# The gate columns of the second block: from 24 split matmuls to eight column-tiled ones and one 0/1 sum

## The reference, cut to what matters

```
def hybrid_layer(x, norm_w, w_in, conv_w, conv_b, gate_bias, ret_norm_w, mlstm_norm_w, w_out):
    h = rmsnorm_2(x, norm_w)                       # x: 256 tokens of 1024
    proj = jnp.matmul(h, w_in)
    (aq, ak, av, ag, bq, bk, bv, bg, cq, ck, cv, co, cg, ci, cf) = jnp.split(proj, cuts, axis=-1)
    ...
    i_pre = ci.transpose(0, 2, 1) + gb[:C_HEADS][None, :, None]    # 4 columns
    f_pre = cf.transpose(0, 2, 1) + gb[C_HEADS:][None, :, None]    # 4 columns
    yc = mlstm(..., i_pre, f_pre)
```

## Time and profile before

| | us |
|---|---|
| median of 3 runs | 901.94 |
| lowest and highest | 900.82, 901.98 |
| the profiled execution | 900.98 |
| its span, first to last instruction | 899.7 |

### The profile page before, as it was taken

One profiled execution on the slowest core, in us unless ns is written; L12 is line 12 of the kernel. 1 busy time (PEld: TensorE's weight loads), 2 busy tenths in 40 slices (PEclk: granted clock), 3 DMA queues, 4 the chain that ended last, 5 costly groups with the idle time before them and its releaser, 6 DMA issues.

```text
span 899.7 us, 12205 instructions
## 1 busy us (share of the span) xinstructions
PE 855.5 (95%) x5030; PEld 554.2 (62%) x5030; DVE 416.4 (46%) x814; ACT 302.0 (34%) x548; POOL 10.3 (1%) x14
## 2 busy tenths in 40 slices
PE   5999999999998989899989899999999999999997
PEld 3668875344454334444444243489978999897985
DVE  3196964011210112001111011089898888989875
ACT  4253133111111111101111011174746666566663
POOL 0001000000000000000000000000100000010000
PEclk9999999999999999999999999999999999999999
DMA  9999989999999999999999999963425444653432
GB/s 371 424 428 427 402 351 428 410 428 428 427 429 428 426 428 427 428 426 428 428 428 427 428 422 423 402 245 123 168 86 187 142 164 180 180 154 105 179 141 71
DMA packets 34857, 292.96 MB, mean 326 GB/s; under 512 B 11376, under 2 KB 11888, under 8 KB 12912
## 3 DMA queue, kind: packets, MB, share of 16 engines
q1 hardware_dynamic: 34800, 292.16, 79.5%
HBM read 290.05 MB, written 1.05 MB: 324 GB/s over the span
## 4 chain that ended last, share of the span: by engine, by line
PE 71%; DMA 24%; DVE 3%; ACT 1%; SPq 1%; issue 1%; ACTq 0%
PE bank L1494 20%; PE bank L1042 16%; DMA more<-in_expert_w 14%; PE bank L1073 8%; DMA ring<-in_expert_w 7%; PE bank L1518 5%; PE bank L409 3%; DMA ring<-in_ada_w 3%; PE bank L1537 2%; PE bank L972 2%; DVE X L379 2%; PE bank L1013 2%; PE bank L452 2%; PE bank L425 1%; PE bank L1694 1%; PE bank L1720 1%
## 5 line engine op out<-in xcount | busy, mean ns | idle before, releaser
L1042 PE MATMUL bank<-ring,xg 128*64 128x512 f32 x760 | 234.5, 605 | 12.8 <-DMA ring<-in_expert_w 12.8
L1494 PE MATMUL bank<-HH,halves 128*128 128x256 f32 x848 | 164.0, 289 | 0.0
L1042 PEld LDWEIGHTS bank<-ring,xg 128*64 128x64 f32 x760 | 76.6, 139 | 123.1 <-issue 98.4
L1494 PEld LDWEIGHTS bank<-HH,halves 128*128 128x128 f32 x848 | 135.4, 192 | 4.6 <-issue 3.5
L1042 PE MATMUL bank<-more,xg 128*64 128x512 f32 x256 | 118.1, 614 | 7.5 <-DMA more<-in_expert_w 7.5
L1494 PE MATMUL bank<-HL,halves 128*128 128x256 f32 x424 | 120.3, 284 | 0.0
L1073 PE MATMUL bank<-ring,X 128*64 128x512 f32 x384 | 114.3, 595 | 0.7 <-ACT X L1113 0.7
L1160 DVE TENSOR_TENSOR X<-X,bank 128x512 f32<-128x512 f32 x16 | 11.0, 688 | 224.2 <-PE bank L1042 224.2
L1384 DVE TENSOR_TENSOR halves<-raw,halves 128x1024 fp32r<-128x1024 f32 (+1 forms) x84 | 91.9, 1128 | 6.4 <-ACT halves L1376 6.3
L1173 DVE SCALAR_TENSOR_TENSOR ygL<-bank,small,ygH 128x512 fp32r<-128x512 f32 x32 | 24.0, 750 | 136.2 <-ACT ygH L1120 136.2
L1494 PEld LDWEIGHTS bank<-HL,halves 128*128 128x128 f32 x424 | 81.6, 193 | 0.8 <-issue 0.5
(11 more groups left out here) (369 smaller groups left out, 1217.9 us busy)
## 6 DMA issues: line engine op xcount, KB each, us to landing
ring<-in_expert_w SPq DMA_DIRECT2D x63, 2048.0 KB, 26.9
more<-in_expert_w SPq DMA_DIRECT2D x22, 2048.0 KB, 26.2
raw<-in_units SPq DMA_DIRECT2D x38, 1024.0 KB, 4.9
ring<-in_ada_w SPq DMA_DIRECT2D x10, 2048.0 KB, 20.9
ring<-in_expert_w SPq DMA_DIRECT2D x17, 1024.0 KB, 28.1
ring<-in_w_in SPq DMA_DIRECT2D x3, 2048.0 KB, 34.7
more<-in_ada_w SPq DMA_DIRECT2D x2, 2048.0 KB, 27.7
ring<-in_w_out SPq DMA_DIRECT2D x2, 2048.0 KB, 22.0
```

What stands on the lines that cost most here:

```text
L1042: t = pe.matmul(bank[3 + i][64 * x:64 * x + 64, :], xg[q % 2][:, k, o + 64 * x:o + 64 * x + 64], w[:, k, :], start=k == 0, stop=k == 7)
L1494: t = pe.matmul(ps[:, T * j:T * j + T], part(x[:, k, 128 * j:128 * j + 128]), part(y[:, k, :]), start=first and a == 0, stop=last and a == ...
```

## The change

The weights of `U_ROWS` no longer go through `high` and `low`. The unit is 292 floats a partition in place of 1024: eight blocks of 32 columns (the eight gate columns and zeros) and a matrix of 36 columns of zeros and ones. DVE multiplies the 256 weights by the norm weight in place (`gate_weigh`). PE multiplies them in plain fp32 with x itself: eight matmuls, block `k` in column tile `k % 4`, so that each of four groups of 32 partitions of the bank holds the sum over two blocks (`gate_parts`). ACT copies this to `X1` (`gate_copy`), and one fp32 matmul with the 0/1 matrix adds the four groups and puts `ci` on rows 0 to 3 and `cf` on rows 32 to 35, in the bank's other half (`gate_sums`). `gate_chain` reads them there.

```
@@ PIECES
-          [(u, i) for i in range(0 if l else 1, 4) for u in (0, 1)] + [(U_ROWS, 0)]
+          [(u, i) for i in range(0 if l else 1, 4) for u in (0, 1)]
@@ second_pe
+                def gate_parts(l):
+                    w = gate_weights(l)[0]
+                    ps = start(l, U_ROWS)
+                    pe.wait_ge(s_gw, l + 12)
+                    if l:
+                        pe.wait_ge(s_xo, 4)
+                    else:
+                        pe.wait_ge(s_add, 8)
+                    for k in range(8):
+                        o = 32 * (k % 4)
+                        t = pe.matmul(ps[o:o + 32, 0:T], w[:, k, :], xT[:, k, :], start=k < 4, stop=k >= 4, tile_position=(0, o))
+                    t.then_inc(s_gcT, 1)
+
+                def gate_sums(l):
+                    pe.wait_ge(s_gabs, 5 * l + 1)
+                    pe.matmul(unit_bank(l, U_ROWS)[0:36, T:2 * T], gate_weights(l)[1], X1[:, 1, 0:T], start=True, stop=True).then_inc(s_unit, 1)
...
+                    gate_parts(l)
                     spread_pe(11 if l else 6, 0)
+                    gate_sums(l)
                     pe.wait_ge(s_hl, 8 * l + 8)
-                    tile(l, 2, 0)
                     tile(l, U_CO, 0)
@@ second_act
+                def gate_copy(l):
+                    act.wait_ge(s_gcT, 2 * l + 1)
+                    act.activation(X1[:, 1, 0:T], unit_bank(l, U_ROWS)[:, 0:T], ACT.Copy).then_inc(s_gabs, 1)
...
                         scale_root(mean, s_rs, 3)
+                        gate_copy(l)
                         high(l, 5)
...
-                        high(l, 2)
+                        high(l, 1)
                         scale_root(bank[6][:, 0:2], s_st2, 2)
+                        high(l, 4)
+                        gate_copy(l)
                         high(l, 5)
@@ second_dve
+                def gate_weigh(l):
+                    w = gate_weights(l)[0]
+                    scale = col("nw2", 8, 8) if l else gw
+                    dve.wait_ge(*unit_arrival(NU * l + U_ROWS))
+                    dve.tensor_tensor(w, w, scale.unsqueeze(2).broadcast_to([128, 8, 32]), ALU.mult).then_inc(s_gw, 1)
...
-                    dve.tensor_tensor(ri, unit_bank(l, U_ROWS)[0:4, 0:T], rs[0:4, :], ALU.mult).then_inc(s_gate, 1)
-                    dve.tensor_tensor(rf, unit_bank(l, U_ROWS)[32:36, 0:T], rs[32:36, :], ALU.mult).then_inc(s_gate, 1)
+                    dve.tensor_tensor(ri, unit_bank(l, U_ROWS)[0:4, T:2 * T], rs[0:4, :], ALU.mult).then_inc(s_gate, 1)
+                    dve.tensor_tensor(rf, unit_bank(l, U_ROWS)[32:36, T:2 * T], rs[32:36, :], ALU.mult).then_inc(s_gate, 1)
...
                     one = scale(l)
+                    gate_weigh(l)
                     if l == 0:
                         low(l, 3)
                         take(one, 3)
                     else:
-                        low(l, 2)
+                        low(l, 1)
                         take(one, 1)
```

More of the change, by code:

```diff
@@ L2619 @@
         "fnr": np.broadcast_to(i["final_norm_w_2"].reshape(1, 1024), (128, 1024)),
[L2620 to L2621 removed]
+        "units": np.stack([np.concatenate([loads(a, [(at, T) for at in UNITS[:U_ROWS]]), rows[None],
+                                           loads(a, [(at, T) for at in UNITS[U_ROWS + 1:]]),
+                                           loads(b, [(T * u, T) for u in range(4)])]) for a, rows, b in zip(w_in_2, gate_rows, i["w_out_2"])]),
     }
```

39 lines of the change are left out of this document (20 added, 19 removed).

## The result

The changed kernel takes 904.09 us (median of 19 runs, 902.41 to 906.15). The kernel before, on the same chips, takes 902.27 (19 runs, 900.16 to 903.58). The ratio is 1.0023, with a 95% interval from 1.0016 to 1.0029: 2.1 us slower, at least 1.4 and at most 2.6.

The account below looks back on a forecast made before the run. The second block's middle was taken to be bound by when `rs` comes from PE's spread. Layer 0 +0.95 (or +0.2) and layer 1 +0.8 gave +1.75 or +1.0; between them +1.4, 903.3 us, own range 902.4 to 904.3.

Parts of the forecast that it names:

- what bounds the middle of each layer: Second block: when `rs` comes from PE's spread; from there some 53.8 us of VectorE and ScalarE work have a fixed length.
- layer 0: With the clock falling, `rs` comes 1.2 us later, the 0.29 us wait goes, PE has 0 in hand: +0.95 us.
- the case of "+0.2": Layer 0 if the clock does not fall there: parts run to 605.3, +0.2 us in place of +0.95.
- the parts: Eight column-tiled fp32 matmuls added on PE ahead of the spread: 1.0 us at full clock, bounds 0.85 and 1.2.
- layer 1: At full clock `rs` comes 1.0 us later and PE had 0.22 us in hand: +0.8 us.
- had in hand: Layer 1, at `by_token` of unit 10: a gap of 0.37 us against layer 0's 0.15 gives PE 0.22 us.
- ScalarE's copy: Copy of the parts, 0.36 us; in layer 1 behind two high halves, PE waits 0.35 us: cost nothing.
- the case with the fall: Both layers' total with the clock at half near layer 0's spread: +1.75 us; +1.0 us without.
- PE-bound after all: Rival: the 0.15 us gaps are modelling and PE's gain of 1.4 us a layer comes through, 899.1 us; 6%.
- The clock falls once more: Rival: clock at half when layer 1's parts start, +1.5 us on `rs`, 904.8 us; 8%.
- The tiles do not overlap: Rival: the parts' column tiles follow one another, 3.72 in place of 1.0 in each layer, 908.7 us; 3%.
- The change does nothing: Rival: unseen slack absorbs the spread's delay and PE's gain is lost in the same waits, 901.9 us; 8%.

Follow-up runs that it names:

- three_of_24: Kernel before with only 3 of the 24 gate products made in each layer (gates not the reference's): 902.16 us, ratio 1.0003.
- copy_sooner: Changed kernel with ScalarE's gate copy of layer 1 ahead of the high halves of units 4 and 3: 909.81 us, ratio 1.0091.
- products_behind: Changed kernel with 24 products of a unit 3 tile made once more in each layer, behind `gate_sums`: 906.33 us, ratio 1.0043.
- both_layers: Changed kernel, spread ahead of parts, layer 0 low half ahead of `rs` copy, layer 1 spread amid units 0 and 1's last products, unit 3 halves earlier: 901.59 us.
- both_layers_2: both_layers with ScalarE's gate copy of layer 1 behind one high half of unit 4 in place of three: 900.39 us, ratio 0.9984.
- before_both: Kernel before, gates still as 24 split products, with the reordering of both_layers: 902.92 us, ratio 1.0008.
- spread_first: Changed kernel with the spread ahead of the parts on PE in place of behind them: 902.57 us, ratio 1.0004.
- copy_after_one: Changed kernel with ScalarE's gate copy of layer 1 behind one high half of unit 4 in place of three early pieces: 903.66 us, ratio 1.0017.
- parts_twice: Changed kernel with the eight column-tiled matmuls of the parts made twice, ahead of the spread: 904.98 us, ratio 1.0038.

## Why the prediction came out as it did

**Right: what bounds the middle of each layer.** The fixed run of VectorE and ScalarE work from the copy of `rs` to `by_token` stood in layer 1 of nine of the 13 kernels, at 52.62 to 52.85 us: all but the four that add products behind the spread or bring `rs` sooner there. It stood with 2.5 us a layer of PE's products fewer (three_of_24) as with `rs` 5.4 us later (copy_sooner). Where it grew, in products_behind (54.50), both_layers (55.09), both_layers_2 (54.23) and before_both (54.09), VectorE's rows show new waits inside it. And in all 13 kernels, in both layers, `by_token` of unit 10 starts 0.14 or 0.15 us behind the end of VectorE's low half, so that half released it every time. The products that were taken away were worth nothing, as the sum had it.

**Right: layer 0.** `by_token` was forecast 0.95 us later and is 1.00 us later. `rs` came 1.39 us later (forecast 1.24), the 0.29 us wait ahead of the gate chain went as forecast, and the stretch got 0.1 us shorter still. That the sum is out by only 0.05 us is in part luck, since misses of 0.15 us on `rs` and 0.1 on the stretch offset each other. The clock did fall in this execution. A window of the kernel after (stretch, length, busy time of PE, PE's weight loads, VectorE, ScalarE and GpSimd, PEclk, DMA):

```profile
606.60:609.90 3.30, 3.30 (x23) 1.69 (x21) 0.75 (x3) 0.69 (x3) 0.00 (x0) 0.50 0.00 0
```

The granted clock is half, the 1.2 GHz level, over the parts and the spread, which is why the parts took 1.87 us. The forecast had the fall end before the parts were done, and the spread at full clock. In the four executions without a fall there, the case of "+0.2" can be read in part: the changed kernel's front gives `rs` at 19.09 (products_behind), spread_first's at 18.74, so the parts cost 0.35 us on `rs` in that case. The kernel before was not caught without a fall, so its `by_token` in that case is not known.

**Right: the parts.** 1.00 us at full clock, as taken between 0.85 and 1.2.

**Mis-sized: layer 1, +1.14 us where +0.8 was forecast.** Two terms failed. The first is the 0.22 us that PE "had in hand". I took it from the chain, where `by_token` starts at 810.95. TensorE's own timeline of the kernel before has it start sooner:

```profile
809.83 1.12 PE L1677 MATMUL bank<-scr,late 128*128 128x512 f32 x2
810.73 0.70 PE L1518 MATMUL bank<-halves,HH 128*128 128x512 f32 x2
```

The low half that it waits for ends at 810.58, 0.15 us before 810.73, the same gap as in layer 0. A piece of the chain starts where the modelled end of the matmul ahead of it lies (809.83 + 1.12 = 810.95), and 810.95 was such an end. PE had nothing in hand. The second is the way from products to parts and back to the spread, which the forecast held to be in the 1.0 us of the parts: it costs 0.08 us ahead of them and 0.11 behind, +0.2 in all. With both the sum would have been 1.2 us; 1.14 was measured.

**Wrong, but without a cost: ScalarE's copy.** The step said "two of the four high halves stand ahead of it" and PE waits 0.35 us. It stands behind three, and PE waited 1.02 us. ScalarE's timeline of the kernel after, layer 1:

```profile
760.48 2.95 ACT L1380 ACTIVATE halves<-early 128x1024 fp32r<-128x1024 f32 x3 [3.05 <-PE bank L1496]
763.33 0.36 ACT L1863 ACTIVATE X<-bank 128x256 f32<-128x256 f32 x1
```

The order printed ahead of the prediction has these three halves in a row, and I costed two. That the cost is nothing held; copy_after_one shows it. PE's waits in layer 0 were forecast at 2.3 us and are 1.63. The clock is not the reason: copy_sooner has the same three waits at full clock (1.05, 0.35 and 0.22). Two short ones ahead of `norm_mean` and `by_token` bring the sum to 1.81, and VectorE's run, shorter by 0.39 us, leaves that much less to wait; the rest stays open.

**The forecast itself** lay between the case with the fall, +1.75, and the one without, +1.0. With the two terms put right these are +2.2 and +1.4, and the measured ratio says +2.1. Both lie so near to 0.2% that "no difference that can be told" and "slower" should have had even chances; the result is slower by just over it, and I had given the smaller chance to that. In the two profiled executions, both with the fall, the block is 0.37 us further apart than the forecast of +1.75, and layer 1 has 0.34 us of that. The rest of the way from +1.4 to +2.1 is the choice of a middle between two cases. That the ratio comes to the case with the fall need not mean that the clock fell in most runs.

**The rivals.** "PE-bound after all" is refuted by three_of_24 and spread_first. "The clock falls once more" did not happen at layer 1's parts, which took 1.00 us. "The tiles do not overlap" is refuted by the same row. "The change does nothing" is refuted by the interval of the ratio (1.0016 at least); of everything in the change but the order, spread_first shows that it is worth nothing that can be told.

What stays open: how often the clock falls near layer 0's spread in executions without a profile, and so whether the measured +2.1 us hold one case or a mixture.

## What to carry to other kernels

Where two engines arrive at a point within a few tenths of a microsecond, the share of the chain by engine names only one of them: follow the other one back from that point, and cost every instruction that comes ahead of the start of its run at full price and everything behind it at nothing, up to a slack that has to be found by adding work: the first engine's waits told too little of it here (1.63 us against 2.28 in layer 0, 0.33 against 1.03 in layer 1), because a third engine stood between. Before a smaller piece of work is put into the place of a larger one, ask if it need stand there: here the parts ahead of the spread cost 2.1 us and behind it 0.4, with an interval from -0.5 to 1.2. Read the start of a matmul that waits from the engine's timeline, not from a piece of the chain; a chain that is all PE does not show that PE is the bound, as products_behind and both_layers_2 have it. And read an order of instructions by count, not by memory.

## What the runs showed of the hardware that was not expected

- A second set of the eight column-tiled fp32 matmuls costs 0.83 to 0.86 us, while the first, with what it takes to switch, costs 1.00 us (parts_twice against the kernel after). A further 0.08 us lie between the last full-array product and the first column tile (0.20 from start to start, where it was 0.12 to the spread), and 0.11 between the start of the full-array matmul behind them and the copy of its result (0.74 where it was 0.63). The forecast had both within the 1.0 us.
- The granted clock was at half near layer 0's spread in the profiled executions of nine of the 13 kernels and at full clock in those of the other four (spread_first, products_behind, parts_twice, copy_sooner). Of four kernels with the same instructions up to there, it fell in after and copy_after_one, and not in products_behind and copy_sooner. So the fall is not set by the order of instructions alone. It is worth about 1.5 us on `rs` in the changed kernel, 20.64 and 20.62 in block time with it, 19.09 and 19.08 without, and 0.5 us with the spread at its old place: 19.25 in the kernel before with it, 18.74 in spread_first without.
